# Inverting the recurrence's triangular systems as compact 32x32 blocks, both directions per step

## The chip, the cores and the metric

The kernel runs as one program on one core of a Trainium2 chip. The metric is the device time of one execution in microseconds (us). The core has a matrix engine (PE, with PEld for its weight loads), a vector engine (DVE), an activation engine (ACT), a general engine (POOL) and a queue for transfers (SP). Each engine works through its own list of instructions in the order in which they were issued. One engine waits for another through semaphores, counters that an instruction raises as it ends.

## The reference

A backbone of two layers runs 128 context tokens and 256 latent tokens through SwiGLU blocks, layer norms and a mixer with three branches: grouped attention, differential attention and a bidirectional recurrence (RWKV-7). The change is in the third branch:

```python
def _rwkv_scan(S0, r, w, kk, a, k, v, reverse):
    def step(S, inp):
        r_t, w_t, kk_t, a_t, k_t, v_t = inp
        sa = jnp.einsum('bhvk,bhk->bhv', S, -kk_t)
        S = S * w_t[:, :, None, :] + sa[..., None] * (kk_t * a_t)[:, :, None, :] + v_t[..., None] * k_t[:, :, None, :]
        return S, jnp.einsum('bhvk,bhk->bhv', S, r_t)
...
    for d in range(2):
        a_h, w_h = heads(a), heads(decay)
        S, o = _rwkv_scan(state0[:, d].astype(f32), rh, w_h[:, :, d], kk, a_h[:, :, d], k_h[:, :, d], vh, reverse=(d == 1))
```

There are eight heads of 64 channels, and each direction has its own decay and rate. The outputs are the two token streams, new keys and values of both attentions and the recurrence's state.

## The kernel before

The recurrence isn't run token by token. Time is cut into six chunks of CH = 64 tokens (NQ = 6), the eight heads into four tiles of two (NB = 4, tile j holds heads on partitions 0 to 63 and 64 to 127). Within a chunk the dependence of each token on the earlier ones of the chunk is a triangular system, and the kernel computes its 64x64 inverse. The chunks of a tile are then chained by four scan steps with that inverse. For one tile there are 6 chunks x 2 directions x 2 heads = 24 systems.

For each tile, in each of the two layers, the work is:

- `gram(j, p)`, p = 0 to 3: three chunks of one direction each. PE multiplies keys with queries and keys into two banks, `own` and `swapped`; ACT copies one half of each `own` block to `lt` (L1981, "the gram copy"); DVE masks the rest into `gr` (L2730, L2732).
- `turn_tok`: PE turns keys into token order; ACT copies them.
- The inverse, which is built level by level. `first_level` (DVE L2741) masks `lt` with the pattern of blocks of size 1; `turn_start` (PE) transposes that; `first_level_done` (DVE L2747, L2750) adds the identity to both forms, `xi` (the inverse) and `xt` (its transpose). Then come levels n = 1 to 5, for blocks of 2, 4, 8, 16 and 32. Per level and direction: POOL masks `lt` into `ltm` (L2246, 384 columns); PE multiplies `ltm` with `xi` (`lx_quads`); ACT copies the result to `tl` (L1991); PE multiplies once with `xt` (`u_quads`, for `xi`) and once the other way round (`ut_quads`, for `xt`); DVE adds the first to `xi` (`add_u`, L2756) and the second to `xt` (`add_ut`, L2766, or the copy L2764 at the last level). The last level needs `xt` alone.
- The scan of the tile before (s = j - 1), four steps of `scan_right`, `scan_solve`, `scan_update`, put between the pieces above, and that tile's group norm (`tile_sums`, `tile_var`, `tile_gate`).
- The preparation of the next tile (j + 1): decays and rates (PE L1342 and L1352, ACT L1928 and L1937), sums (DVE L2681), exponentials (ACT L1961 to L1974), keys and queries (DVE L2699, L2708, L2714, L2715), decayed keys (DVE L2722, L2723).

A matrix product on 64x64 blocks is issued by `quads` (L1309): one matmul for each of the two heads, each on its own rows of the array, both into one bank. In the trace each float32 matmul leaves two records. The two directions of a level are staggered: while one is in its copy or its addition, PE works on the other (`level_lx0_u1`, `level_u0_lx1`, `level_ut`):

```python
def level_u0_lx1(j, n):
    u_ready(j, n, 0)
    lx_ready(j, n, 1)
    for q in range(NQ):
        uu = u_quads(j, n, 0, q) if n < NL else ut_quads(j, n, 0, q)
        lx = lx_quads(n, 1, q)
```

The order of the work on each engine is written out by hand in the loop `for j in range(NB)`, once for each engine. Nothing reorders it, so a copy or an addition that stands behind others in that list waits for them. Outside the recurrence the kernel is dense 128x128 matmuls (L905 to L907) on weights that stream in.

Of the kernel before, what the change touches and what calls it, by code (L numbers as in the profile page):

```python
# [17 lines left out]
ALU = mybir.AluOpType  # L18
# [59 lines left out]
CO_MASK = CO_LEV + 2 * len(LEVELS) * CH  # L78
# [6 lines left out]
def shape_constants():  # L85
# [19 lines left out]
    for d in range(2):  # L105
        a, b = (s, t) if d == 0 else (t, s)
        for n, size in enumerate(LEVELS):
            m = (a // (2 * size) == b // (2 * size)) & (a // size % 2 == 0) & (b // size % 2 == 1)
            o = CO_LEV + (2 * n + d) * CH
            c[:, o:o + CH] = m  # L110
# [5 lines left out]
    c[:, CO_ID64:CO_ID64 + CH] = s == t  # L116
    for g in range(32):
# [139 lines left out]
def build(nc, I, O):  # L257
# [17 lines left out]
        "lt_ready": 16, "ltm_ready": 40, "max_done": 48, "merged_done": 16, "n_ready": 24, "o_done": 4, "o_read": 4,  # L275
# [6 lines left out]
        "tile_sum": 6, "tl_done": 40, "tl_ready": 40, "tok_ready": 16, "tok_sums": 6, "tok_t": 16, "u_done": 32,  # L282
        "ut_done": 40, "var_ready": 3, "vt_done": 1, "vtok_ready": 4, "vtok_t": 4, "weighted_done": 24, "xf_ready": 24,
        "xhi_ready": 32, "xi_ready": 40, "xi_t": 8, "xm_ready": 32, "xt0_ready": 8, "xt_ready": 48, "z_ready": 8}
# [12 lines left out]
    with glob:  # L297
# [78 lines left out]
        with ExitStack() as mix:  # L376
# [27 lines left out]
            with ExitStack() as ph:  # L404
# [5 lines left out]
                with ExitStack() as same:  # L410
# [8 lines left out]
                tl = sb("tl", [128, 2 * NQ, CH], ctx=ph)  # L419
# [13 lines left out]
                ksq = (guc[:, 0, :], guc[:, 1, :], tl[:, 0:NQ, :].rearrange("p q s -> p (q s)"),  # L433
                       tl[:, NQ:2 * NQ, :].rearrange("p q s -> p (q s)"))
# [46 lines left out]
        ltm_ready, xt0_ready, xt_ready, xi_t, xi_ready = (  # L481
            sem(n) for n in ("ltm_ready", "xt0_ready", "xt_ready", "xi_t", "xi_ready"))
        tl_done, tl_ready, u_done, ut_done = (sem(n) for n in ("tl_done", "tl_ready", "u_done", "ut_done"))
# [2518 lines left out]
```

## Time and profile before

| what | value |
|---|---|
| median of 3 runs | 2526.09 us (2523.46 to 2530.59) |
| profiled execution, first to last instruction | 2519.7 us |
| median less that span | 6.4 us |
| PE busy | 2379.6 us (94%), 23632 matmul records |
| DVE busy | 1368.0 us (54%) |
| ACT busy | 1031.8 us (41%) |
| POOL busy | 342.1 us (14%) |
| chain that ended last | PE 84%, DVE 9%, issue 2%, ACT 2% |

The page gives the span of the profiled execution and no further time of it, so the 6.4 us are what lies around the span, as far as that execution was like the median one. The shares of busy time are averages over the whole program: the recurrence fills some 190 us of each layer, from 718 to 912 us in layer 1 and from 1957 to 2151 us in layer 2, and there the engines stand differently to one another than in the dense parts.

### The profile page before, as it was taken

How to read it: one execution, taken by the hardware profiler on the slowest of the kernel's cores; microseconds unless marked ns; L12 is line 12 of the kernel's file. 1: busy time of each engine (PE TensorE's matmuls, PEld its weight loads, DVE VectorE, ACT ScalarE, POOL GpSimd, SP SyncE). 2: the span in 40 equal slices, each digit the busy share in tenths (PEclk: the TensorE clock that was granted, in tenths of full speed). 3: DMA queues.
4: the chain of work that ended last, by engine and by line, in shares of the span. 5: the costliest groups of instructions: out<-in, count | busy, mean ns of one | idle time of the engine just before them, and what ended most of it. 6: DMA issues, size and time to landing. Idle time of an engine off the chain costs nothing.

```text
span 2519.7 us, 56070 instructions
## 1 busy us (share of the span) xinstructions
PE 2379.6 (94%) x23632; PEld 2228.4 (88%) x23632; DVE 1368.0 (54%) x2301; ACT 1031.8 (41%) x1677; POOL 342.1 (14%) x330
## 2 busy tenths in 40 slices
PE   6999999999988889999999999999999788899998
PEld 5899989889977779999988999998899777899998
DVE  3434456477488756344443334655765876554444
ACT  3333244355644435333343333444556343353332
POOL 0000032000033304000120001320000433130002
PEclk8999999999989999999999999999999899999999
DMA  8875634332300023554457765343333000344442
GB/s 286 265 229 177 216 98 134 92 95 85 105 15 4 29 56 114 172 176 125 150 179 237 221 186 182 99 114 91 95 85 92 3 4 29 89 117 128 127 120 86
DMA packets 468550, 309.32 MB, mean 123 GB/s; under 512 B 15330, under 2 KB 427468, under 8 KB 468172
## 3 DMA queue, kind: packets, MB, share of 16 engines
q1 hardware_dynamic: 468032, 305.65, 40.4%
q8 instruction: 187, 3.06, 0.5%
q14 instruction: 63, 0.52, 0.1%
q10 hardware_dynamic: 268, 0.09, 0.0%
HBM read 302.30 MB, written 3.41 MB: 121 GB/s over the span
## 4 chain that ended last, share of the span: by engine, by line
PE 84%; DVE 9%; issue 2%; ACT 2%; DMA 1%; POOL 1%; SPq 1%; DVEq 0%; ACTq 0%; POOLq 0%
PE acc L905 22%; PE acc L906 21%; PE acc L907 21%; PE pb L1309 4%; PE acc L1309 2%; PE pb L982 2%; PE pb L990 1%; DMA raw<-in_ffn_w_in 1%; PE pb L1236 1%; PE pb L997 1%; DVE w_lo L2328 1%; DVE merged L2631 1%; PE pb L905 1%; DVE gr L2732 1%; PE acc L969 0%
## 5 line engine op out<-in xcount | busy, mean ns | idle before, releaser
L905 PE MATMUL acc<-xm_hi,w_hi 128*128 128x384 f32 x2288 | 784.5, 343 | 28.7 <-DVE xm_lo L2338 24.4
L2328 DVE TENSOR_TENSOR w_lo<-raw,w_hi 128x1024 fp32r<-128x1024 f32 (+2 forms) x432 | 533.9, 1236 | 509.5 <-ACT w_hi L1733 501.0
L907 PE MATMUL acc<-xm_hi,w_lo 128*128 128x384 f32 x2288 | 771.3, 337 | 0.0
L906 PE MATMUL acc<-xm_lo,w_hi 128*128 128x384 f32 x2256 | 760.6, 337 | 0.0
L1733 ACT ACTIVATE w_hi<-raw 128x1024 fp32r<-128x1024 f32 (+2 forms) x432 | 446.2, 1033 | 316.1 <-PE acc L907 224.0
L905 PEld LDWEIGHTS acc<-xm_hi,w_hi 128*128 128x128 f32 x2288 | 434.7, 190 | 59.8 <-issue 49.0
L907 PEld LDWEIGHTS acc<-xm_hi,w_lo 128*128 128x128 f32 x2288 | 434.3, 190 | 0.0
L906 PEld LDWEIGHTS acc<-xm_lo,w_hi 128*128 128x128 f32 x2256 | 428.9, 190 | 0.5
L905 PE MATMUL acc<-h_hi,w_hi 128*128 128x384 f32 x704 | 238.9, 339 | 0.0
L907 PE MATMUL acc<-h_hi,w_lo 128*128 128x384 f32 x704 | 237.1, 337 | 0.0
L906 PE MATMUL acc<-h_lo,w_hi 128*128 128x384 f32 x704 | 237.1, 337 | 0.0
L1768 ACT ACTIVATE sa<-acc 128x384 f32<-128x384 f32 x88 | 43.3, 492 | 428.9 <-PE acc L907 428.7
L2192 POOL TENSOR_TENSOR ln_sum<-x 128x384 f32<-128x384 f32 x12 | 17.6, 1470 | 879.4 <-DVE x L2354 879.2
L905 PEld LDWEIGHTS acc<-h_hi,w_hi 128*128 128x128 f32 x704 | 132.4, 188 | 5.0 <-issue 5.0
L906 PEld LDWEIGHTS acc<-h_lo,w_hi 128*128 128x128 f32 x704 | 132.4, 188 | 0.0
L907 PEld LDWEIGHTS acc<-h_hi,w_lo 128*128 128x128 f32 x704 | 132.4, 188 | 0.0
L2440 DVE TENSOR_TENSOR hf<-sa,acc 128x384 f32<-128x384 f32 x88 | 48.8, 555 | 145.9 <-PE acc L907 138.3
L2246 POOL TENSOR_TENSOR ltm<-lt,cst 128x384 f32<-128x384 f32 x80 | 83.7, 1047 | 145.1 <-PE pb L1309 86.4
L2354 DVE SCALAR_TENSOR_TENSOR x<-acc,modv,x 128x128 f32<-128x128 f32 x88 | 32.7, 413 | 108.3 <-PE acc L907 108.1
L1309 PE MATMUL pb<-xi,ltm 64*64 64x64 f32 x1920 | 79.2, 229 | 11.0 <-POOL ltm L2246 4.7
L1309 PE MATMUL pb<-xt,tl 64*64 64x64 f32 x1920 | 79.8, 223 | 5.9 <-issue 5.8
L1991 ACT ACTIVATE tl<-pb 128x384 f32<-128x384 f32 x80 | 39.2, 491 | 111.8 <-PE pb L1309 111.5
(394 smaller groups left out, 3472.9 us busy)
## 6 DMA issues: line engine op xcount, KB each, us to landing
raw<-in_ffn_w_in SPq DMA_DIRECT2D x176, 512.0 KB, 4.1
modw<-in_w_mod SPq DMA_DIRECT2D x69, 1024.0 KB, 6.4
raw<-in_w_in SPq DMA_DIRECT2D x114, 512.0 KB, 4.1
raw<-in_ffn_w_out SPq DMA_DIRECT2D x64, 512.0 KB, 3.8
raw<-in_w_up SPq DMA_DIRECT2D x24, 512.0 KB, 3.6
raw<-in_ffn_w_out SPq DMA_DIRECT2D x26, 384.0 KB, 3.2
raw<-in_w_out SPq DMA_DIRECT2D x16, 512.0 KB, 4.0
modx<-in_w_mod SPq DMA_DIRECT2D x3, 1024.0 KB, 9.3
```

The costliest lines, as they stand in the source:

```text
L905: pe.matmul(out, lhs[0], rhs[0], start=first, stop=False)
L906: pe.matmul(out, lhs[0], rhs[1], start=False, stop=False)
L907: return pe.matmul(out, lhs[1], rhs[0], start=False, stop=last)
L982: mm = pe.matmul(pb[2 if late else 1][32 * k:32 * k + 32, :], cond_at(Q - (LATE_Q if late else PRE_Q), 4 * r + k), slot[:, k, :], start=r ...
L1309: mm = pe.matmul(out[HALVES[1 - i] if cross else hp], lhs[hp], rhs[hp], start=start, stop=stop, skip_group_check=True)
L1733: done(act.activation(w_hi[:, c % SPL, 0:w], raw[:, c % RAW, 0:w], ACT.Copy), hi_done)
L1768: freed(l, act.activation(sa[:, j % 2, :], gbank(ka)[:, 0:TOK], ACT.Silu), ka)
L1991: done(act.activation(tl[:, NQ * d:NQ * d + NQ, :].rearrange("p q s -> p (q s)"), lx_bank(n, d)[:, 0:TOK], ACT.Copy), tl_ready)
L2246: done(pool.tensor_tensor(ltm[:, u, :], lt[:, u, :], over(cst[:, o:o + CH], NQ), ALU.mult), ltm_ready)
L2328: done(dve.tensor_tensor(w_lo[:, c % SPL, 0:w], raw[:, c % RAW, 0:w], w_hi[:, c % SPL, 0:w].bitcast(F32), ALU.subtract), lo_done)
L2354: ins = dve.scalar_tensor_tensor(out=x[:, m, a:b], in0=gbank(key)[:, a:b], scalar=modv[:, 3 * s + 2, m, gi:gi + 1], in1=x[:, m, a:b], op0= ...
L2440: freed(l, dve.tensor_tensor(hf[:, j % 2, :], sa[:, j % 2, :], gbank(kb)[:, 0:TOK], ALU.mult), kb)
```

## The change

The 64x64 inverse is no longer built in five levels of 64-wide blocks. Only its two 32x32 diagonal blocks are, in four levels; the remaining off-diagonal block ("the corner") is made by two more products at the end.

- **Blocks.** `xi`, `xc` (the transpose, in the place of `xt` during the levels), `ltm` and `tl` are 32 columns wide for each chunk instead of 64. A bank of 384 columns holds all 12 chunks of both directions, so a level is one product (`level_lx`, 48 matmuls of 32x32x32), one ACT copy, one product (`level_u`, 48 matmuls), one DVE addition, and one DVE transpose of 32x32 blocks (`STREAM_TRANSPOSE`), which takes the place of the second product (`ut_quads`) and its addition. The four matmuls of a chunk lie on four different 32-row groups.
- **First level.** DVE masks, adds the identity and transposes, 192 columns each, for each direction. `turn_start` and `first_level_done` are gone.
- **Masks.** POOL makes those of all four levels at once: for each direction one operation of 192 and one of 576 elements a partition.
- **Corner.** PE `corner_first` (24 matmuls), ACT copy of 192 columns, PE `corner(j, 0)` and `corner(j, 1)` (24 each), an ACT copy of 192 columns each; POOL `place` writes the diagonal blocks to `xt` with zeros beside them (2 operations).
- **Gram.** The half of `own` that is inverted is issued as 32-wide pieces: 24 matmuls for each `gram` instead of 12.
- **Order.** On every engine's list the pieces of both directions fall together.

For one tile that makes 456 matmuls of the inverse in the place of 384, and 96 in the place of 48 in the grams. On DVE, 14 operations (six of 192 columns, eight of 384) stand in the place of 24 of 384. On ACT, 4 copies of 384 and 3 of 192 columns stand in the place of 10 of 384. On POOL, 4 masks (1536 elements a partition in all) and 2 placings stand in the place of 10 masks (3840 elements).

```diff
-LEVELS = (1, 2, 4, 8, 16, 32)
+BL = CH // 2
+LEVELS = (1, 2, 4, 8, 16)
 NL = len(LEVELS) - 1
+XR = NL + 2
+QUARTERS = tuple(slice(32 * g, 32 * g + 32) for g in range(4))
...
-                xi = sb("xi", [128, 2 * NQ, CH], ctx=ph)
-                ltm = sb("ltm", [128, 2 * NQ, CH], ctx=ph)
+                xc = sb("xc", [128, 2 * NQ, BL], ctx=ph)
+                xi = sb("xi", [128, 2 * NQ, BL], ctx=ph)
+                ltm = sb("ltm", [128, NL, 2 * NQ, BL], ctx=ph)
...
-                            quads(own[:, at], bt[:, d, q * CH:(q + 1) * CH], both, True, True)
+                            quads(own[:, 2 * CH * e + CH:2 * CH * e + 2 * CH], bt[:, d, q * CH:(q + 1) * CH], ar[:, j % 2, d, q, 1, :],
+                                  True, True)
...
+                    def blocks(out, lhs, rhs):
+                        for g in QUARTERS:
+                            mm = pe.matmul(out[g], lhs[g], rhs[g], start=True, stop=True, skip_group_check=True)
+                        return mm
+                    def level_lx(j, n):
+                        if n == 1:
+                            pe.wait_ge(gram_read, since(l, gram_read, 4 * j + 4))
+                        pe.wait_ge(ltm_ready, since(l, ltm_ready, 4 * j + (3 if n == 1 else 4)))
+                        pe.wait_ge(xi_ready, since(l, xi_ready, XR * j + n + 1))
+                        for u in range(2 * NQ):
+                            mm = blocks(pb[0][:, u * BL:(u + 1) * BL], ltm[:, n - 1, u, :], xi[:, u, :])
+                        mm.then_inc(tl_done, 1)
+                    def level_u(j, n):
+                        pe.wait_ge(tl_ready, since(l, tl_ready, NL * j + n))
+                        pe.wait_ge(xt_ready, since(l, xt_ready, XR * j + n + 1))
+                        for u in range(2 * NQ):
+                            mm = blocks(pb[2][:, u * BL:(u + 1) * BL], xc[:, u, :], tl[:, u, :])
+                        mm.then_inc(u_done, 1)
...
-                    def level_lx(j, n, d):
-                        act.wait_ge(tl_done, since(l, tl_done, 2 * NL * j + 2 * (n - 1) + d + 1))
+                    def level_lx(j, n):
+                        act.wait_ge(tl_done, since(l, tl_done, NL * j + n))
+                        done(act.activation(tl[:, :, :].rearrange("p u s -> p (u s)"), pb[0][:, 0:2 * NQ * BL], ACT.Copy), tl_ready)
...
+                    def masks(j, d):
+                        pool.wait_ge(lt_ready, since(l, lt_ready, 4 * j + 2 * d + 2))
+                        for n0, n1 in ((1, 2), (2, NL + 1)):
+                            form = [128, n1 - n0, NQ, BL]
...
-                    def add_ut(j, n, d):
...
+                    def add_u(j, n):
+                        whole = xi[:, :, :].rearrange("p u s -> p (u s)")
+                        dve.wait_ge(u_done, since(l, u_done, NL * j + n))
+                        done(dve.tensor_tensor(whole, whole, pb[2][:, 0:2 * NQ * BL], ALU.add), xi_ready)
+                        done(dve.transpose(xc[:, :, :].rearrange("p u s -> p (u s)"), whole), xt_ready)
...
-                        for n in range(2, NL + 1):
-                            level_lx0_u1(j, n)
-                            level_ut(j, n - 1, 1)
...
-                            level_u0_lx1(j, n)
-                            level_ut(j, n, 0 if n < NL else 1)
+                        level_u(j, 2)
+                        if nxt:
+                            prepare_norm(j + 1)
+                        level_lx(j, 3)
+                        if old:
+                            tile_sums(s)
+                        level_u(j, 3)
```

ACT's list in tile 1, from the copy of `tl` at level 1 to the one at level 2 (`aa<-acc` are the next tile's rates, `osum` the scan's output, `zi` and `eh` exponentials of the next tile, `sld` a state). Before:

```order
L1991 ACTIVATE tl<-pb 128x384
L1961 ACTIVATE cs<-zi 128x384
L1966 ACTIVATE sg<-sg 128x384
L2008 ACTIVATE sld<-acc 128x2x64
L1937 ACTIVATE aa<-acc,half_bias 128x384 x2
L2004 ACTIVATE osum<-acc 128x384
L1991 ACTIVATE tl<-pb 128x384
L1970 ACTIVATE zi<-zi 128x384
L1974 ACTIVATE eh<-lam 128x6
L1991 ACTIVATE tl<-pb 128x384
```

and now:

```order
L1991 ACTIVATE tl<-pb 128x384
L1960 ACTIVATE cs<-zi 128x384
L1965 ACTIVATE sg<-sg 128x384
L2016 ACTIVATE sld<-acc 128x2x64
L1936 ACTIVATE aa<-acc,half_bias 128x384 x2
L2012 ACTIVATE osum<-acc 128x384
L1969 ACTIVATE zi<-zi 128x384
L1973 ACTIVATE eh<-lam 128x6
L1991 ACTIVATE tl<-pb 128x384
```

The exponentials of `zi` and `eh` stood between the level's two copies; now they stand ahead of its only one. The two rates stand ahead of it as before.

PE's list in the same tile, from the scan's last update to the second product of level 3:

```order
L1320 MATMUL acc<-gr,sas 64x64 x4
L1415 MATMUL pb<-xi,ltm 32x32 x48
L1363 MATMUL acc<-cmix,lora_a 128x384 x2
L1415 MATMUL pb<-tl,xc 32x32 x48
L1178 MATMUL acc<-cst,ln_st 64x128 x6
L1415 MATMUL pb<-xi,ltm 32x32 x48
L1563 MATMUL acc<-osum,cst 128x384
L1566 MATMUL acc<-guc,cst 128x384
L1415 MATMUL pb<-tl,xc 32x32 x48
```

Before, the rates `acc<-cmix,lora_a` (whose results ACT's `aa<-acc` takes) stood ahead of the first product of level 2; they now stand behind it.

## Rows read from the trace of the kernel before

**Rows 1.** Stretches: span, busy PE, PEld, DVE, ACT, POOL (instructions), clock, DMA share, GB/s

```profile
783.40:806.70 23.30, 20.62 (x712) 17.35 (x709) 18.75 (x35) 13.77 (x26) 11.42 (x12) 1.00 0.02 5
874.30:895.80 21.50, 18.80 (x644) 16.63 (x634) 10.46 (x20) 7.36 (x13) 6.00 (x6) 0.92 0.25 78
```

**Rows 2.** Chain that ended last, in order of time, tiles 1 and 3: start, us, what

```profile
783.05 0.85 PE acc L1352 x4
...
785.44 0.81 PE acc L1167 x12
786.24 0.84 PE acc L1562 x2
787.09 0.65 PE acc L1565 x2
...
801.08 0.57 DVE xt L2766
...
881.25 1.94 issue
```

**Rows 3.** Whole program, groups by line, with mean ns of one instruction

```profile
L2246 POOL TENSOR_TENSOR ltm<-lt,cst 128x384 f32<-128x384 f32 x80 | 83.7, 1047 | 145.1 <-PE pb L1309 86.4 <-issue 39.7 <-ACT lt L1981 16.4
...
L2766 DVE TENSOR_TENSOR xt<-xt,pb 128x384 f32<-128x384 f32 x72 | 39.9, 554 | 8.8 <-PE pb L1309 5.5
L1991 ACT ACTIVATE tl<-pb 128x384 f32<-128x384 f32 x80 | 39.2, 491 | 111.8 <-PE pb L1309 111.5
```

**Rows 4.** Timeline of PE, products of one level: start, us, instruction, count

```profile
744.21 0.22 PE L1309 MATMUL pb<-tl,xt 64*64 64x64 f32 x2
744.23 0.23 PE L1309 MATMUL pb<-xi,ltm 64*64 64x64 f32 x2
744.27 0.23 PE L1309 MATMUL pb<-tl,xt 64*64 64x64 f32 x2
...
744.86 0.87 PE L1309 MATMUL pb<-xt,tl 64*64 64x64 f32 x24
```

**Rows 5.** Timeline of PE's weight loads at the same place

```profile
744.11 0.14 PEld L1309 LDWEIGHTS pb<-tl,xt 64*64 64x64 f32 x2 [0.17 <-issue]
744.12 0.14 PEld L1309 LDWEIGHTS pb<-xi,ltm 64*64 64x64 f32 x2
744.16 0.14 PEld L1309 LDWEIGHTS pb<-tl,xt 64*64 64x64 f32 x2
```

**Rows 6.** Timeline of DVE, tiles 1 and 3

```profile
797.46 0.65 DVE L2714 TENSOR_TENSOR gg<-eh 128x5 f32<-128x5 f32 x1
...
857.68 1.33 DVE L2741 TENSOR_TENSOR xt<-lt,cst 128x384 f32<-128x384 f32 x1
```

**Rows 7.** Timeline of ACT, tile 1, around level 2

```profile
783.97 1.19 ACT L1937 ACTIVATE aa<-acc,half_bias 128x384 f32<-128x384 f32 x2 [0.58 <-PE acc L1352]
...
786.24 0.52 ACT L1970 ACTIVATE zi<-zi 128x384 f32<-128x384 f32 x1
```

**Rows 8.** Gram copies of ACT: the last one of tiles 0, 1 and 3

```profile
732.90 0.33 ACT L1981 ACTIVATE lt<-pb 128x192 f32<-128x192 f32 x1 [2.55 <-PE pb L1309]
...
774.41 0.33 ACT L1981 ACTIVATE lt<-pb 128x192 f32<-128x192 f32 x1 [2.46 <-PE pb L1309]
...
866.24 0.33 ACT L1981 ACTIVATE lt<-pb 128x192 f32<-128x192 f32 x1 [1.54 <-PE pb L1309]
```

**Rows 9.** Timeline of DVE: where tiles 0, 1 and 3 are through

```profile
762.34 0.36 DVE L2730 TENSOR_TENSOR gr<-pb,cst 128x192 f32<-128x192 f32 x1
...
806.67 0.36 DVE L2730 TENSOR_TENSOR gr<-pb,cst 128x192 f32<-128x192 f32 x1
...
895.22 0.56 DVE L2764 COPY xt<-pb 128x384 f32<-128x384 f32 x1
```

**Rows 10.** Stretches of 3 us where the clock falls; columns as in Rows 1

```profile
729.00:732.00 3.00, 1.53 (x32) 1.38 (x32) 2.83 (x6) 0.49 (x1) 0.00 (x0) 0.50 0.00 0
...
858.00:861.00 3.00, 1.29 (x42) 1.29 (x44) 2.83 (x6) 0.24 (x2) 0.59 (x1) 0.82 0.00 0
```

More of the change, by code:

```diff
@@ L534, in gram_banks, with side, on_diagonal @@
             return (pb[2], pb[3]) if p % 2 == 0 else (pb[0], pb[1])
-        def lx_bank(n, d):
-            return pb[d + 2 * (1 - n % 2)]
-        def u_bank(n, d):
-            return pb[d + 2 * (n % 2)]
+        def side(d):
+            return slice(NQ * d, NQ * d + NQ)
+        def on_diagonal(d):
+            return lt[:, side(d), BL * d:BL * d + BL]
         def gbank(key):
@@ new lines, in level_u, with corner_first @@
+                    def level_u(j, n):
[4 more added lines that the diff above has]
+                        mm.then_inc(u_done, 1)
+                    def corner_first(j):
+                        pe.wait_ge(xi_ready, since(l, xi_ready, XR * j + XR))
+                        for q in range(NQ):
+                            for d in range(2):
+                                for h in range(2):
+                                    of, to = QUARTERS[2 * h + d], QUARTERS[2 * h + 1 - d]
+                                    mm = pe.matmul(pb[0][to, q * BL:(q + 1) * BL], lt[of, NQ * d + q, BL * (1 - d):BL * (1 - d) + BL],
+                                                   xi[of, NQ * d + q, :], start=True, stop=True, skip_group_check=True)
+                        mm.then_inc(corner_t, 1)
@@ new lines, in corner @@
+                    def corner(j, d):
+                        pe.wait_ge(corner_ready, since(l, corner_ready, 3 * j + 1))
+                        pe.wait_ge(xt_ready, since(l, xt_ready, XR * j + XR))
+                        for q in range(NQ):
+                            for h in range(2):
+                                of, to = QUARTERS[2 * h + 1 - d], QUARTERS[2 * h + d]
+                                at = slice(q * BL, q * BL + BL)
+                                pe.matmul(pb[1 - d][to, at], toff[of, q, :], xc[of, NQ * d + q, :], start=True, stop=True,
+                                          skip_group_check=True)
+                                mm = pe.matmul(pb[1 - d][of, at], cst[of, CO_ID32:CO_ID32 + BL], xc[of, NQ * d + q, :],
+                                               start=True, stop=True, skip_group_check=True)
+                        mm.then_inc(corner_t, 1)
@@ L1629, in _ @@
                             scan_right(s, 1)
-                        turn_start(j, 0)
-                        if old:
                             scan_solve(s, 1)
@@ L1655, in _ @@
                             scan_update(s, 3)
+                        level_lx(j, 2)
                         if nxt:
@@ L2120, in _ @@
                             exp_halves(g1)
-                        level_lx(j, 5, 1)
+                        corner(j, 0)
+                        corner(j, 1)
                         if old:
@@ L2284, in _ @@
                             decay(2 * j + 3)
-                        for n in range(1, NL + 1):
-                            mask(j, n, 0)
-                            mask(j, n, 1)
-                            if n == 3 and nxt:
-                                rate(2 * j + 2)
-                                rate(2 * j + 3)
-                            if n == 4 and nxt:
-                                keys(2 * j + 2)
+                        masks(j, 0)
+                        masks(j, 1)
                         if nxt:
+                            rate(2 * j + 2)
+                            rate(2 * j + 3)
+                            keys(2 * j + 2)
                             keys(2 * j + 3)
+                        place(j, 0)
+                        place(j, 1)
                         if old:
@@ new lines, in first_level @@
+                        link(dve.tensor_tensor(mine, on_diagonal(d), over(cst[:, o:o + BL], NQ), ALU.mult))
+                        done(dve.tensor_tensor(mine, mine, over(cst[:, CO_ID32:CO_ID32 + BL], NQ), ALU.add), xt_ready)
+                        done(dve.transpose(xi[:, side(d), :].rearrange("p q s -> p (q s)"), mine.rearrange("p q s -> p (q s)")), xi_ready)
+                    def add_u(j, n):
[3 more added lines that the diff above has]
+                        done(dve.transpose(xc[:, :, :].rearrange("p u s -> p (u s)"), whole), xt_ready)
```

239 lines of the change are left out of this document (82 added, 157 removed).

## The prediction

> **What bounds the kernel now.** The dense parts are untouched, so I read only the recurrence, and first by stretches: in tile 1 of layer 1 the levels take 23.3 us in which DVE is busy for 18.75 us and PE for 20.62 us [rows 1]. Both are nearly full, so the second view decides, the chain that ended last. It runs mostly over PE up to 797 us, and from there to 813 us over DVE alone, one 0.57 us operation after the other, the level additions among them [rows 2]. So in the second half of a tile DVE is the bound, and PE, busy as it looks, waits for it. In tile 3, which has no next tile to prepare, DVE is busy for only 10.46 us of 21.5 [rows 1]: there the chain product, copy, product, addition sets the time.
>
> I price the stretch from the last gram copy of a tile to the first masking that belongs to the next one. Before, it is 774.41 to 806.67 = 32.3 us in tile 1, 732.90 to 762.34 = 29.4 us in tile 0, and, to the last write of `xt`, 866.24 to 895.78 = 29.5 us in tile 3 [rows 8, 9].
>
> **What a step on PE costs.** The new product has 48 matmuls, 96 records, on four row groups. Now four 64x64 parts of the array are in use when two directions are issued together: pairs of records start at 744.21, .23, .27, so four records each 58 ns, 14.6 ns a record [rows 4]. A part is thus renewed every 58 ns for 64 columns. With two parts only, 24 records take 0.87 us with 0.22 us of tail: 27 ns a record, 55 ns a part [rows 4]. The time is per part and goes with the columns, so for 32 columns I take half, 29 ns a part, 7.3 ns a record with four parts: 96 x 7.3 = 0.70 us, with the tail **0.95 us**. The upper bound is that a record doesn't come faster than the 14.6 ns seen: 96 x 14.6 = 1.40, with tail **1.65 us**. Which one depends on how fast PE can issue. For the fast end speaks the start of a burst: four weight loads begin within about 0.02 us, then none for 0.04 us [rows 5], so the loads wait for the array and not for the issue. I take 0.95 us. Both are at the clock of 2.4 GHz.
>
> **The sum for tile 1**, from the last gram copy:
> - First level. DVE masks gram in 0.95 us, then three operations of 192 columns at 0.36 (192 columns from the bank: 0.36 [rows 9]) = 1.1. POOL has a mask of 192 and one of 576 elements; at 1.05 us for 384 [rows 3] that is 0.5 + 1.6 us, starting with the copy, and a masking of `lt` on DVE beside POOL took 1.33 us [rows 6], where 0.56 is usual. I take 0.8 us of waiting, and 0.45 for copy and semaphores: **3.3 us**.
> - Four levels, each two steps (1.9), a copy of 0.49 + 0.06 [rows 3], an addition of 0.55 + 0.05 (as L2766 [rows 3]): 3.05 x 4 = **12.2 us**. The transpose isn't in it: it comes after the addition, which alone the next product needs, and is over while that product and its copy run. Its cost shows in no row; I take that of a 384-column addition, 0.56; half of that changes nothing, and up to 1.5 us stays covered.
> - PE's other work in the list. Rate 0.85, norm 0.81, sums 0.84 + 0.65 [rows 2], and the scan's last steps and the tile's variance, 2.5 us by my reading of the list. Of these 5.7 us the part behind a product whose copy is awaited is hidden, 0.55 us each four times: **3.5 us**.
> - ACT's queue at level 2. The copy now stands behind the two rates (1.19), the scan's output (0.49), and the exponentials `zi` and `eh` (0.52 [rows 7] and, for 6 columns, some 0.2), and the rates can begin only after PE's 0.85, which stands behind the product. Product to copied is then 0.85 + 1.19 + 0.49 + 0.73 + 0.49 + 0.2 = 3.95 us instead of 0.55: **3.4 us**, of which the 0.85 is already counted above: **2.6 us**.
> - DVE's tail after level 4: from 797.46 to 806.67 it never idles and runs five level operations of 0.57 there [rows 6, 9]; the other 6.3 us stay: **6.3 us**, with the last transpose 0.6 ahead. The corner (2.3 us on PE and ACT: 72 matmuls, 1.1 us with tails, three copies of about 0.35) lies beside this tail and costs nothing; without the tail it would cost its 2.3.
> Sum 28.5 us against 32.3: **-3.8 us**. Tile 2 has the same list: -3.8.
>
> **Tile 0** has no scan and no norm of an old tile (3.3 us less), but the clock is at half where its levels begin (0.50 at 729 to 732 us [rows 10]), which I price at +1.9: 27.1 against 29.4, **-2.3**. **Tile 3** has neither rates nor next keys: 3.3 + 12.2 + 3.0 of other PE work + 0.8 of ACT's queue + corner 2.3 = 21.6; of the 29.5 before some 2.5 are PE waiting for nothing that the profile shows (1.94 in one piece [rows 2]), while the weights' stream returns (DMA share 0.25 over the stretch [rows 1]), and I leave them in: 24.1, **-5.4**. In the half of a tile before the last gram copy `turn_start` leaves PE's chain (-0.7), the gram gets 24 more records (+0.35) and the first level grows from 0.57 to 1.1 us on DVE (+0.45): nothing.
>
> A layer gives -15.3, two layers -31. Against it stands the **clock**: in the row at 858 us PE was busy for 1.29 of 3 us, and in it the granted clock fell from 2.4 to 1.2 GHz (mean 0.82) [rows 10]. After the change PE waits about 3 us for ACT's queue in each of tiles 0 to 2. I allow one such fall in each tile, 1.4 us each: +11. So **-20 us**: the profiled span of 2519.7 goes to 2500, and the median of 2526.1, which lies 6.4 above that span, to **2506 us**.
>
> **The rivals.**
> - *Issue sets the pace* (1.65 us a step). Eight steps x 0.7 = 5.6 us a tile, 45 us in all, less 10 that fall into waits anyway; PE is busier then, so without the falls of the clock: -31 + 35 = +4, **2530 us**. For it: 14.6 ns is the fastest sustained pace the trace shows, and every step has 192 instructions. Against it: rows 5. It decides from about 13 ns a record. A middle pace of 11 ns gives about 2518.
> - *The clock falls and stays*, the case on the other side. PE now stands still in every level for copy and addition, 1.15 us of 3.05. If the clock falls to 1.2 GHz in the levels, each step costs 0.65 more (5.2 us a tile) and the grams, scans and norms on the chain about 5 us more; in all eight tiles +80, in the six without tile 0's slow start, for two thirds of the time, +40: 2526 - 31 + 40 = **2535 us**. For it: at 729 us PE was busy for 1.53 of 3 us and the clock stood at 0.50 [rows 10]. Against it: in the levels of tile 1, where PE waited between products too, it stood at 1.00 throughout [rows 1].
> - *Row groups take turns.* If four 32-row parts don't run side by side but as slowly as the two-part rows (27 ns a record), a step is 2.8 us, 1.85 more, eight a tile: +118 - 31 = **2613 us**. Against it: in rows 4 and 5 the two heads' matmuls, on different rows and into one bank, start together. The Trainium skill, "TensorE: Matmul & The Clock Gate", section on the 56 ns, says that matmuls never start less than about 25 ns apart however few columns they have. By that rule a step would be 96 x 25 = 2.4 us and the kernel slower; the trace disagrees as far as records on different parts go (14.6 ns), and agrees with it if it is meant for one part (29 ns).
> - *The chain moves to something I hold for covered*, DVE against POOL's long mask, or the corner. Each microsecond a tile costs 8; with three, **2526 us**, no change.
>
> **How the numbers follow.** Main case 0.56 (2492 to 2518 by its bounds: the fall of the clock between 0 and 1.5 times a tile, step 0.9 to 1.2 us); issue pace 0.17; clock 0.09; turns 0.04; cover lost 0.14. A measurement of this kernel tells about 0.3%, 7.6 us, from no change. Faster: the main case, and a part of the others, 0.60. Same: cover lost and part of issue pace, 0.19. Slower: the rest, 0.21. The range takes in the main case, cover lost and issue pace: 2488 to 2534; outside are the turns and half of the clock's case.
>
> **What would show it.** Right: 32x32 records that start 7 to 8 ns apart, a step of 0.9 to 1.0 us; DVE busy 6 to 7 us less a tile; PE idle in tile 1 with ACT's copy of `tl` as releaser, about 3 us at level 2; chain no longer on DVE between level 1 and 4. Wrong: records 14 ns or more apart; a granted clock of 0.50 over whole tiles; a transpose longer than 1.5 us; `gr` of the next tile waiting for the corner.

## The result, and the profile after

The changed kernel takes **2604.94 us** (median of 4 runs, 2603.72 to 2610.7), the kernel before 2526.90 us in the same comparison; the ratio is 1.031 (95% interval 1.0295 to 1.0326). I had forecast 2506 us, faster. The profiled execution spans 2604.3 us against 2519.7.

The recurrence holds nearly the whole difference. In layer 1 it takes 39.2 us more; in layer 2, from the first gram masking to the end of the last tile, 246.3 us (from 2000.27) against 202.1 (from 1959.18), 44.2 us more; the spans differ by 84.6. First the kernel before (the whole stage of layer 1, then tile 1), columns as in [rows 1]:

```profile
718.40:919.80 201.40, 169.80 (x5640) 149.32 (x5640) 145.27 (x272) 79.49 (x162) 64.72 (x68) 0.95 0.07 18
762.34:806.67 44.33, 38.89 (x1404) 34.06 (x1404) 35.74 (x69) 21.13 (x43) 16.44 (x18) 1.00 0.02 4
```

The changed kernel, the same two, then the levels of tile 1 alone, from the first LX product to the corner's first:

```profile
718.70:959.30 240.60, 180.20 (x6600) 149.27 (x6600) 118.99 (x232) 71.73 (x150) 42.84 (x52) 0.75 0.06 16
769.15:825.03 55.88, 41.95 (x1654) 34.10 (x1650) 29.31 (x58) 19.20 (x40) 11.24 (x14) 0.81 0.02 4
789.70:816.26 26.56, 18.27 (x893) 14.96 (x891) 9.14 (x18) 9.43 (x19) 4.40 (x6) 0.82 0.02 4
```

DVE lost the 6.4 us a tile that I expected, and it isn't the bound any more. But PE has 250 records more in tile 1, and the mean granted clock of the stage fell from 0.95 to 0.75. Against [rows 8, 9]: from the last gram copy (783.87) to the next tile's masking (825.03) it now takes 41.2 us, where it took 32.3 and I forecast 28.5. The 12.7 us too few are 2.5 at the first level, 8.3 in the levels, 1.9 at the end. The part of the tile ahead of that stretch, which I had put at no change, takes 14.7 us (769.15 to 783.87) against 12.1 [rows 8, 9]. Tiles 0 to 3 of the layer take 6.3, 11.6, 8.0 and 13.2 us more than before, each from its first masking to the next tile's (tile 3 to the end of the stage), where I had forecast 2.3, 3.8, 3.8 and 5.4 less.

PE's products in that stretch, by the timeline (start, length, record, count, in brackets the idle time before and what ended it):

```profile
789.70 1.50 PE L1415 MATMUL pb<-xi,ltm 32*32 32x32 f32 x96
793.53 1.02 PE L1415 MATMUL pb<-tl,xc 32*32 32x32 f32 x96 [1.42 <-ACT tl L1991]
...
797.71 0.67 PE L1415 MATMUL pb<-xi,ltm 32*32 32x32 f32 x55 [0.33 <-issue]
...
809.02 1.02 PE L1415 MATMUL pb<-tl,xc 32*32 32x32 f32 x96
810.85 1.10 PE L1415 MATMUL pb<-xi,ltm 32*32 32x32 f32 x96
812.60 0.37 PE L1415 MATMUL pb<-tl,xc 32*32 32x32 f32 x19
814.53 1.01 PE L1415 MATMUL pb<-tl,xc 32*32 32x32 f32 x77 [1.56 <-issue]
```

A step takes 1.02 us at 2.4 GHz (forecast 0.95) and 1.50 at 1.2 GHz. Two kinds of gap stand between: those that another engine ends, and two in the middle of a step, "issue": idle time for which the profile shows nothing that was waited for. Level 2 waited 3.17 us for ACT's copy, as I had foreseen (about 3). DVE's and ACT's timelines in tile 1 show the masked product beside POOL's long one, which I had allowed for, and the square root behind the corner, for which DVE waited and which I had not.

```profile
785.28 1.33 DVE L2751 TENSOR_TENSOR xc<-lt,cst 128x192 f32<-128x192 f32 x1
...
822.20 0.19 DVE L2807 RECIPROCAL gnr<-gnr 128x6 f32<-128x6 f32 x1 [2.37 <-ACT gnr L2025]
```

```profile
820.54 1.28 ACT L2025 ACT_TABLE_LOAD   x1
821.84 0.27 ACT L2025 ACTIVATE gnr<-acc,lam 128x6 f32<-128x6 f32 x1
```

The clock in stretches of 3 us; it stands at 1.2 GHz (0.50) where PE did nothing or little, and falls where PE waits for ACT or DVE (in the third row PE had been idle from 799.23 to 802.39, and from 798 to 801 the clock was still 1.00):

```profile
732.00:735.00 3.00, 0.00 (x0) 0.00 (x0) 2.83 (x6) 0.00 (x0) 0.00 (x0) 0.50 0.00 0
744.00:747.00 3.00, 1.22 (x4) 0.07 (x2) 0.00 (x0) 1.63 (x3) 0.00 (x0) 0.50 0.00 0
801.00:804.00 3.00, 1.61 (x98) 1.54 (x100) 0.00 (x0) 2.66 (x6) 0.54 (x2) 0.56 0.00 0
```

Before, 744 to 747 stood at 1.00 with PE busy for 2.74 us.

### The profile page after: what moved, and what is told of

Its sections match the earlier page's. It is cut to its first block, busy times and chain, and to the rows that moved or that the text cites. A ratio compares the mean times of both kernels' runs of the same rounds, so it can differ in the third digit from the quotient of the medians.

```text
span 2604.3 us, 59482 instructions
## 1 busy us (share of the span) xinstructions
PE 2404.0 (92%) x25552; PEld 2232.7 (86%) x25552; DVE 1316.8 (51%) x2221; ACT 1016.6 (39%) x1653; POOL 298.8 (11%) x298
## 3 DMA queue, kind: packets, MB, share of 16 engines
q1 hardware_dynamic: 468032, 305.44, 39.2%
## 4 chain that ended last, share of the span: by engine, by line
PE 87%; DVE 7%; ACT 3%; issue 2%; DMA 1%; POOL 0%; SPq 0%; DVEq 0%; ACTq 0%; POOLq 0%
PE acc L916 22%; PE acc L917 21%; PE acc L918 21%; PE acc L1320 3%; PE pb L1415 3%; PE pb L993 2%; PE pb L1001 1%; PE pb L1320 1%; PE pb L1247 1%; PE pb L1008 1%; PE acc L1178 1%; DVE w_lo L2337 1%; PE pb L916 1%; DVE xc L2751 1%; DVE merged L2640 1%
## 5 line engine op out<-in xcount | busy, mean ns | idle before, releaser
L1415 PEld LDWEIGHTS pb<-tl,xc 32*32 32x32 f32 x3072 | 38.5, 130 | 55.9 <-ACT tl L1991 39.1
L1415 PE MATMUL pb<-tl,xc 32*32 32x32 f32 x3072 | 43.5, 218 | 42.5 <-ACT tl L1991 31.5
L2759 DVE TENSOR_TENSOR xi<-xi,pb 128x384 f32<-128x384 f32 x32 | 17.7, 554 | 128.2 <-PE pb L1415 128.2
L2260 POOL TENSOR_SCALAR sg<-sg 128x384 f32<-128x384 f32 x16 | 8.5, 533 | 525.7 <-ACT sg L1927 524.7
```

Source lines behind the costliest of these rows:

```text
L1415: mm = pe.matmul(out[g], lhs[g], rhs[g], start=True, stop=True, skip_group_check=True)
```

## The experiments

Four theories stood: **A**, the clock at 1.2 GHz; **B**, waits that come from the order of the queues (B2) and from both directions being one step (B1); **C**, the instructions of PE don't arrive fast enough; **D**, POOL's long product slows DVE's first level. Where I give a difference it is between medians. All except the last four are edits of the changed kernel.

**Idle PE filled (e_fill).**

```
+def fill(n):
+    for _ in range(n):
+        pe.matmul(pb[3][:, 384:512], ident, cst[:, 0:128], start=True, stop=True, ...)
 ...
+fill(4)            # 3 to 12 of them in each wait
 level_u(j, 1)
```

> Idle TensorE filled: 20 to 35 extra matmuls a tile (128x128 with 128 columns, into 128 unused columns of a bank, nobody reads them) stand in TensorE's waits between the inverse's steps; every wait, queue and dependency stays as in the changed kernel. Theory A (the clock: the changed kernel's TensorE stands still between serial steps, and the granted clock is at 1.2 GHz in some 119 of the 240 us of a layer's recurrence, where before it was in some 20 of 201): with the waits filled the clock is at 2.4 GHz nearly throughout, a step of 96 records takes 1.02 us everywhere where 1.50 is common now, and the time falls by 25 to 45 us, to 2560 to 2580. Theory B (the serial chain and the order of the queues cost, the clock little): at most 10 us less; 2595 to 2610. If the extra matmuls themselves run past the waits they fill, both are hidden and the time rises: 2610 to 2640.

Measured 2619.99 us (ratio to before 1.0363, 1.0333 to 1.0393), 15 us more: the third of the cases. Its timeline of PE in tile 0:

```profile
750.20 0.86 PE L1415 MATMUL pb<-xi,ltm 32*32 32x32 f32 x78 [0.18 <-issue]
...
754.04 0.67 PE L1415 MATMUL pb<-tl,xc 32*32 32x32 f32 x54 [1.40 <-issue]
...
757.93 0.46 PE L1415 MATMUL pb<-xi,ltm 32*32 32x32 f32 x33 [1.25 <-issue]
...
761.64 0.58 PE L1415 MATMUL pb<-tl,xc 32*32 32x32 f32 x26 [1.76 <-issue]
```

The clock part came true in part: more steps ran at 1.02 us, the mean clock of layer 1's recurrence rose from 0.75 to 0.85 and that of the program from 0.933 to 0.954. The time didn't follow: issue gaps ahead of level products grew from 6.8 to 13.4 us in the layer, in tile 0 one every 3.8 us. Theory A fell as the cause of the whole, and C came up. The test isn't a clean one, as the fillings are instructions too: 216 records more in the layer, by the rate measured below an estimated 12 us in both layers.

**Halves (e_halves), order (e_order), POOL (e_pool).**

```
 def level_lx(j, n):             # e_halves; U, ACT's copy, DVE's addition and transpose alike
-    for u in range(2 * NQ): ... pb[0] ... ; mm.then_inc(tl_done, 1)
+    for d in range(2):
+        for q in range(NQ): ... pb[d] ... ; mm.then_inc(tl_done, 1)
 ...
+level_lx(j, 1)                  # e_order, ACT
 copy_tok(j, 1, 1); scan_right(s, 3)
-level_lx(j, 1)
 ...
+pool.wait_ge(xi_ready, ...)     # e_pool, ahead of the product for levels 2 to 4
```

> One part of the change undone: the blocks stay 32x32 with four levels, corner and transposes, and all other work keeps its place in every queue, but each step is two halves again, one for each direction (48 records, a bank of its own, copy, addition and transpose of 192 columns). Theory B1 (both directions as one step leave nothing to work on while a step's copy or addition is under way): a level's four waits of TensorE (some 0.7 us after the products, 0.7 and more after the addition) are half covered by the other direction, about 1 us a level less, 32 levels: 25 to 40 us from that and some 10 to 20 from the clock, so 2545 to 2575. Theory A alone (clock) would show the same sign, but only with the share of 2.4 GHz up. Rival (the added instructions of ACT and DVE, each with a fixed cost, and the queue waits decide): 2600 to 2615.

> The change kept whole, only the order of independent work altered: ACT's copy of level 1 ahead of the ktok and rs copies, that of level 2 ahead of the two rate activations and the output copy, the square root and its two table loads ahead of the corner; on DVE the third scan copy ahead of the second direction's first level; on TensorE the root's expansion ahead of the next tile's first gram part. Theory B2 (the waits that came from queue order cost what the trace shows of them: 2.8 us at the first level, 1.4 less 0.7 at level 1, 3.2 less 0.7 at level 2, 1 to 2 at the tile's end, in three tiles of four): 5 to 7 us for each of six tiles, 30 to 42 us less: 2562 to 2575. Theory A: the clock stays as it is since the time between steps is as empty as before, 15 us at most: 2590 to 2605.

> Only POOL's long mask product of each direction (576 columns, 1.55 us) waits until DVE's first level of that direction is done; nothing else is altered. Theory D (the first masked product on DVE takes 1.33 to 1.53 us in place of 0.36 because POOL's long product runs beside it, and all of it lies on the path to level 1): DVE's L2751 falls to about 0.4 us, 1 us for each of eight tiles, 5 to 9 us less: 2596 to 2600. If the product is not on the path, or POOL's later end delays level 2 or the rates: no difference, 2602 to 2608.

Measured: e_halves 2608.13 (1.0309, 1.0291 to 1.0326), no gain, as its rival said; B1 fell as a cause by itself. e_order 2581.92 (1.0205, 1.0187 to 1.0222), 23 us less where B2 wanted 30 to 42. e_pool 2598.00 (1.0274, 1.0258 to 1.0289), 7 us less, as D said; the masked product on DVE, by its line (minimum, median, maximum in ns), in the changed kernel and in e_pool:

```profile
L2751 DVE TENSOR_TENSOR xc<-lt,cst x16: 357/1076/1526, 726.7 to 2183.7; 128x192 f32<-128x192 f32 x16
```

```profile
L2753 DVE TENSOR_TENSOR xc<-lt,cst x16: 357/359/831, 724.6 to 2176.3; 128x192 f32<-128x192 f32 x16
```

In e_order the waits for ACT's `tl` went and issue gaps stood in their place, in the level steps of tile 1:

```profile
790.92 0.59 PE L1415 MATMUL pb<-tl,xc 32*32 32x32 f32 x46 [1.58 <-issue]
...
802.76 0.26 PE L1415 MATMUL pb<-xi,ltm 32*32 32x32 f32 x8 [2.59 <-issue]
```

The level stretch of tile 1 in e_fill, e_halves and e_order, against 26.56 us for 893 records, hardly moves, whatever wait is taken out:

```profile
794.87:821.93 27.06, 23.19 (x937) 19.78 (x936) 9.52 (x19) 9.43 (x19) 5.29 (x7) 0.88 0.02 4
```

```profile
787.68:815.17 27.49, 19.13 (x892) 15.60 (x890) 10.66 (x26) 10.12 (x23) 4.77 (x6) 0.75 0.02 4
```

```profile
786.70:813.24 26.54, 19.72 (x891) 16.09 (x891) 10.82 (x22) 12.46 (x24) 4.83 (x6) 0.77 0.02 4
```

**Instructions fewer and more.** e_wide makes each level block with two 64x64 weights, e_extra adds 48 one-column products to a wait, e_cut takes 48 products a tile out of the gram half and the corner (POOL and ACT take over a part), e_order_pool joins the two that helped.

```
-mm = blocks(pb[0][...], ltm[:, n - 1, u, :], xi[:, u, :])      # e_wide
+mm = quads(pb[0][...], ltm[:, n - 1, v:v + 2, :]..., xi[:, u, :], True, True)
 ...
+for _ in range(2 * NQ):                                        # e_extra, before level_u(j, 2)
+    blocks(pb[3][:, 384:385], cst[:, 0:BL], cst[:, 0:1])
```

> Work changed so that the output is not the reference's: in the level steps each 32-column block is made by 2 products of 64x64 weights instead of 4 of 32x32, with the same sources, destinations and waits; a step has 48 records and 48 weight loads instead of 96 and 96. Theory C (TensorE's instructions are the bound: the trace shows them arriving in packets of 16 KB, never closer together than about 3.3 us, some 256 instructions of TensorE each, and idle time before records of one step with nothing waited for, up to 1.8 us): 768 instructions a tile less are 3 packets, 10 us a tile where the supply binds; the idle time put down to issue goes from the level steps, and the time falls by 35 to 70 us, to 2535 to 2570. Theory A+B (clock and serial waits): only the products' own time, some 0.3 us in each of 64 steps, less: 2582 to 2592.

> The opposite: 48 products of one column (32x32 weights, unused target) more in each tile, put behind the second LX step where TensorE waits 3.2 us for ACT's copy anyway; 96 records and 96 weight loads more, about 0.7 us of TensorE. Theory C (instruction supply): 192 instructions are three quarters of a packet, 2.5 us a tile later on, although they stand in a wait: 10 to 22 us more, 2615 to 2627, and more issue time in later steps. Theory A+B: hidden in tiles 1 and 2, 0.7 us in some of the others: 2603 to 2609.

> Fewer instructions of TensorE with the result kept: in the gram half one product of 128 columns as before the change and one 32x32 block written over it (24 products a tile less), and in the corner no products by the identity, POOL copies these rows instead (24 a tile less); 192 instructions a tile less in all, more work on POOL and two more copies on ACT. Theory C: three quarters of a packet a tile, 10 to 20 us less: 2584 to 2595. Theory A+B: TensorE is not the bound there, POOL and ACT have more to do at the tile's end: 2600 to 2612.

> The two that helped together: the altered order of independent work and POOL's long product behind DVE's first level. If their gains add (23 and 7 us): 2573 to 2577. Theory C: what the first frees the instruction supply takes back in part, so less than the sum, 2576 to 2582, with more issue time than in either.

Measured: **e_wide** 2665.19 (1.0531, 1.0509 to 1.0552), a miss and no test: two parts of the array in place of four made a step of 48 records 2.77 us at 1.2 GHz, in place of 1.50. **e_extra** 2624.39 (1.0367, 1.0346 to 1.0387), 19.5 us more for 0.7 us of PE a tile put into a wait of 3.2, within C's 10 to 22. **e_cut** 2605.94 (1.0299, 1.0282 to 1.0315): nothing gained, against C's 10 to 20. **e_order_pool** 2569.69 (1.0158, 1.0136 to 1.0181), 35 us less, where the sum is 30 and C wanted less than the sum: that part of C's forecast missed. The issue gaps did grow, before level products to 17.2 us in a layer against 6.8 in the changed kernel (the waits of PE: total, times, longest):

```profile
PE pb L1415 <- issue: 17.2, 17, 2.3
```

```profile
PE pb L1415 <- issue: 6.8, 7, 1.6
```

**The supply by itself (e_stream).**

```
 if n == 1:
     pe.wait_ge(gram_read, ...)
+    if j == 0:
+        for _ in range(12 * 2 * NQ):
+            blocks(pb[3][:, 384:384 + BL], cst[:, 0:BL], cst[:, 0:BL])
```

> The supply measured by itself: in the first tile of each layer, before level 1, 576 independent products of 32x32 (an unused target, the same shape as a step's, in all twelve steps' worth: 1152 records and 1152 weight loads) that wait for nothing. Theory C (a packet of 16 KB, 256 instructions, at most every 3.3 us): 2304 instructions are 9 packets, so after a first burst at the pace of a step the stretch runs in bursts with issue gaps between, 26 to 30 us in all, and the time rises by 45 to 55 us for the two layers (4.5 us of each stretch lie in a wait): 2650 to 2660. Rival (the pace of the records, 8.4 ns at 2.4 GHz to 12.6 at 1.2 GHz, holds for a long stream too): 12 to 15 us in all, 2620 to 2630.

Measured 2678.07 (1.0584, 1.0568 to 1.06); the stretch runs from 734.56 to 765.5, 31 us where C said 26 to 30 and the rival 12 to 15. In the timeline of PE:

```profile
734.56 3.20 PE L1415 MATMUL pb<-cst 32*32 32x32 f32 x223 [3.25 <-DVE gr L2744]
739.32 1.93 PE L1415 MATMUL pb<-cst 32*32 32x32 f32 x128 [1.56 <-issue]
742.77 1.93 PE L1415 MATMUL pb<-cst 32*32 32x32 f32 x128 [1.52 <-issue]
746.50 1.93 PE L1415 MATMUL pb<-cst 32*32 32x32 f32 x128 [1.80 <-issue]
...
761.14 1.93 PE L1415 MATMUL pb<-cst 32*32 32x32 f32 x128 [1.80 <-issue]
764.87 0.65 PE L1415 MATMUL pb<-cst 32*32 32x32 f32 x33 [1.80 <-issue]
```

and the transfers of the 26 us from 739 to 765 (queue: packets, MB, share):

```profile
q8 instruction: 7, 0.11, 1.9%
```

The same queue over the whole program, in the changed kernel and in e_stream:

```profile
q8 instruction: 202, 3.31, 0.5%
q8 instruction: 220, 3.60, 0.6%
```

This is the cause in its plainest form. After a burst of 223 records come groups of exactly 128, seven of them between the starts at 739.32 and 764.87 (25.55 us), and seven instruction packets of 16 KB: one packet every 3.65 us, **28.5 ns a record**. Over the program e_stream has 2304 records and as many weight loads more than the changed kernel, and 18 packets more: 256 instructions each, which are 128 records and their 128 weight loads. The Trainium skill, "Perfetto Trace Analysis", section on the lifecycle of an instruction, says that instructions are of 64 bytes; 256 of them are 16 KB, and this trace agrees. The time rose by 73 us where C said 45 to 55. In layer 1 tile 0 took 32.8 us more, 29.5 of them ahead of its first level product: the wait that I had set off against the stretch hid about 1.5 us of it and not 4.5. The next tile took 4.3 more. The clock stood at 1.2 GHz in the stretch; but in tile 0's levels it did so in the changed kernel too.

**Combined, and where fewer records help.** e_all is e_order_pool with e_cut, e_gram_cut with its gram part alone, e_all_halves adds the halves to e_all.

> The altered order, POOL's product behind the first level, and the 192 instructions a tile less, together. Theory C: once the queue waits are out of the way TensorE's instructions are what the level steps wait for, so the cut that gained nothing alone now gains three quarters of a packet a tile: 10 to 20 us under the kernel with order and POOL alone, 2550 to 2562. Theory A+B: no more than the products' own time, 0.3 us a tile, and POOL's added copies: 2565 to 2575.

> As the kernel with the altered order and POOL's product moved, with the gram half's 96 instructions a tile less alone (the corner as in the change). Theory C: a third of a packet a tile, 5 to 10 us less than 2570: 2560 to 2566. Rival: nothing, 2567 to 2573.

> The kernel with order, POOL and cut, its steps in halves again by direction. Theory C: the instruction count is the same, so what the halves cover the supply takes back: within 6 us of the kernel without halves. Theory B1: the halves gained nothing alone since queue waits held both directions; without these, 15 to 30 us less.

Measured 2571.25 (1.0166, 1.0151 to 1.0181), 2570.74 (1.0168, 1.0153 to 1.0184) and 2559.34 (1.0123, 1.0106 to 1.014). The cuts failed a second time, against C's forecasts of 2550 to 2562 and 2560 to 2566: they lie in the gram half and the corner, ahead of and behind the levels. PE takes up instructions ahead, but no more than about that burst of 223 records, so what is saved outside a dense stretch doesn't help inside it; that reading fits, no run isolates it. The halves gained 12 us, between what C and B1 said. e_all_halves is the fastest version with 32x32 blocks and the reference's result.

**Half the records within the levels (e_pairs, e_pairs_order, e_before_pairs).** Each product here covers two neighbouring blocks with the weights of the first, so the result isn't the reference's; the columns are the same in all.

```
-for u in range(2 * NQ):
-    mm = blocks(pb[0][:, u * BL:(u + 1) * BL], ltm[:, n - 1, u, :], xi[:, u, :])
+for u in range(0, 2 * NQ, 2):
+    mm = blocks(pb[0][:, u * BL:(u + 2) * BL], ltm[:, n - 1, u, :], xi[:, u:u + 2, :]...)
```

> Work changed so that the output is not the reference's: each product of a level step takes the 64 columns of two neighbouring blocks with the weights of the first, so a step has 48 records of 64 columns in place of 96 of 32, on the same four row groups, with the same columns in all, sources, targets and waits. Theory C (28.5 ns a record with its weight load is what the instructions allow; 893 records in the level stretch of tile 1 took 26.6 us): 384 records a tile less, 10.9 us by that rate, of which 7 to 11 can be had before the chain of copies and additions binds: 55 to 85 us less, 2520 to 2550. Theory A+B (clock, serial waits): the columns are the same, so 0 to 8 us less: 2597 to 2605.

> The same pairs together with the altered order and POOL's product behind the first level. Theory C: without the supply's limit the queue waits count in full, 3 us and more a tile: 20 to 35 us less than with pairs alone, 2490 to 2520, which is what my sum gave for the change. Theory A+B: 2562 to 2570, as without pairs.

> The kernel before with the same device: LX and U products take 128 columns of two neighbouring chunks with the weights of the first, 216 records a tile fewer of 1404, the same columns; its output is not the reference's. If the kernel before also ran close to the supply's rate (31.6 ns a record over tile 1, against 28.5): 2 to 4 us a tile less, 2500 to 2512. If DVE bounds it, as I read from its profile: 2522 to 2529.

Measured: e_pairs 2561.79 (1.0128, 1.0111 to 1.0145), 43 us less, short of 55 to 85; e_pairs_order **2489.60** (0.9843, 0.9828 to 0.9858), 115 us less than the change and 72 less than e_pairs, where 20 to 35 were expected; e_before_pairs 2511.24 (0.9924, 0.991 to 0.9939), 19.5 us under the kernel before. Tile 1's levels in e_pairs_order:

```profile
774.52:791.70 17.18, 13.90 (x506) 10.90 (x506) 11.98 (x22) 10.46 (x22) 4.04 (x5) 1.00 0.02 4
```

and in e_order_pool, the same but for the pairs:

```profile
781.62:806.84 25.22, 16.38 (x891) 13.13 (x891) 11.97 (x22) 12.60 (x24) 6.05 (x7) 1.00 0.02 5
```

Both at 2.4 GHz, with the same DVE work; 385 records fewer make 8.0 us. A paired step takes 0.87 us in place of 1.02, so 1.2 of the 8.0 are the products' own. The same stretch in e_pairs, with half the records and the queues' order as in the change:

```profile
784.00:809.58 25.58, 19.09 (x508) 14.86 (x506) 9.63 (x20) 9.42 (x19) 2.30 (x4) 0.68 0.01 3
```

So C is shown, but it isn't alone. In tile 1 two limits stand at nearly the same height: halving the records alone takes the stretch from 26.56 to 25.58 us, altering order and POOL alone to 25.22, and both together to 17.18. In e_pairs the 3.17 us wait for ACT's copy is still there, and half of the steps run at 1.2 GHz, which is why it fell short. In the whole kernel order and POOL are worth 35 us with all records and 72 with half of them.

**A version that keeps the result (v_turn, v_turn_order, v_turn_apart)**, edits of the kernel before: 64x64 blocks, five levels, UT by DVE.

```
-done(dve.tensor_tensor(mine, mine, lx_bank(n, d)[:, 0:TOK], ALU.add), xt_ready)
+done(dve.transpose(mine, flat(xi, d)), xt_ready)     # levels 1 to 4, level_ut gone there
```

> A version of the kernel before with the reference's result: blocks of 64x64 and five levels as there, but the other orientation of the inverse comes from DVE's transposes of 32x32 blocks (the matrix has only such blocks on its diagonal until the last level), not from products; the products by the identity that start a tile and the crossing of the two heads' halves of the array go too. TensorE has 288 records of 1404 a tile fewer, DVE the same number of operations of 384 columns. Theory C: the kernel before with 216 records fewer gained 19 us, so 12 to 28 us less than before: 2500 to 2515. Against it: the level products lose their four-part mode (27 ns a record in place of 14.6 within a burst), 5 us a tile if the burst's pace and not the supply decides: 2525 to 2560.

> The same with DVE's third scan copy ahead of the second direction's first level, the part of the altered order that can be carried over alone. As it frees TensorE's last scan products from DVE's 1.7 us or more: 1 to 2 us in each of six tiles, 5 to 10 us less than the version without it; if the products then wait for the supply instead, no difference.

> The version with DVE's transposes and altered scan copy, with the reference's result, but LX and U steps issued apart (LX of one direction, LX of the other, U, U), each of 24 records, 0.7 us, so that the copies and additions of one direction lie beside products of the other; ACT's and DVE's work regrouped to match. In v_turn_order a level takes 4.7 us in tile 1 (795.07 to 799.95): two double steps of 1.4 us and two waits of 0.8 to 0.9 us with their tails. Apart, if the waits are covered, 2.9 to 3.4 us a level, four levels, eight tiles: 35 to 55 us less than v_turn_order, 2490 to 2510, below both kernels. If DVE (36 us busy in tile 1 before) or POOL's masks bind instead: 2515 to 2535.

Measured 2551.01 (1.0085, 1.0071 to 1.0099), 2544.33 (1.0055, 1.0042 to 1.0068) and 2535.94 (1.0033, 1.0021 to 1.0045). No product of a level waits for issue, and yet none beats the kernel before; v_turn came out in the case against it, and v_turn_apart 1 us above the worse of its two. In v_turn_order the 48 records of a double step start over 1.4 us, 29 ns each. That is near the 27 ns of two parts of the array [rows 4], the products' own pace and not the supply's; a wait follows:

```profile
795.07 0.33 PE L1309 MATMUL pb<-tl,xt 64*64 64x64 f32 x4 [0.81 <-DVE xi L2736]
...
797.52 0.33 PE L1309 MATMUL pb<-xi,ltm 64*64 64x64 f32 x4 [0.84 <-ACT tl L1975]
```

In v_turn_apart PE waits longest for DVE's scan state `sp` (10.5 us in layer 1), then for DVE's `kt` at the tile's end (6.5) and POOL's masks (5.2). The limit of the supply was taken away; the slower products and the serial chain of copy, addition and mask came in its place, and no run separates the two. I found no version that gives the reference's result and beats both.

## Why the prediction was wrong, by its steps

**What bounds the kernel now.** I read DVE as the bound of a tile's second half and PE as waiting for it. Only half right: 216 records fewer a tile took 19.5 us off the kernel before with DVE unchanged. At 1404 records in 44.33 us, 31.6 ns each, tile 1 already ran close to the 28.5 of e_stream.

**"What a step on PE costs": the step that failed**, though its number was nearly right. 0.95 us was forecast and 1.02 measured, at 8.4 ns a record. But I took the pace of one burst for the pace of a stretch, and from [rows 5] concluded that "the loads wait for the array and not for the issue". That row shows the start of one burst, and e_stream shows that a burst of up to 223 records says nothing of the pace behind it. The row I should have asked for is the instruction queue: packets over a tile against records over a tile.

**"Four levels ... 12.2 us"**, with PE's other work 3.5 and ACT's queue 2.6: 18.3 us by the sum for the levels; 26.56 measured, and 17.18 once the records are half and the order altered. It lacked the line 893 records x 28.5 ns = 25.5 us, or some 23 us with a full burst ahead (e_stream's first 892 records, 734.56 to 757.80); either is larger than all of it. For a whole tile the same line gives 1654 x 28.5 = 47.1 us, above the 40.5 that I forecast for tile 1 (44.3 less 3.8) and above the 44.3 of before. But as a sum of waits and durations it was too small as well: with half the records e_pairs still took 25.58 us there. The price per record isn't to be multiplied out either: by it the 250 records more would be 57 of the 78 us, yet e_cut and e_gram_cut took 96 and 48 of them away and gained nothing. It is a floor of a dense stretch.

**"In the half of a tile before the last gram copy ... nothing"**: 2.6 us more in tile 1 (14.7 against 12.1). I counted 24 records more where a tile's four grams have 96; e_gram_cut, with half of these gone, gained nothing, so the cause of this term stays open.

**First level 3.3 us**: 5.8. DVE's wait beside POOL was in the sum at 0.8 us and showed 0.97 (1.33 against 0.36; e_pool, where POOL's product comes later, has 0.36); not in it was that `scan_update` stands ahead of the first level product on PE and waits for a copy that stands behind DVE's first level (2.8 us at 787.80).

**The corner costs nothing beside the tail**: wrong by 1.9 us a tile. ACT's square root and table load stand behind the corner's copies, and DVE waited 2.37 us for them. Moving these, the two points above and ACT's copies of levels 1 and 2 gave 35 us of the 78 back.

**The clock** was in the sum at 11 us for one fall a tile. It was at 1.2 GHz for about half of the stage (mean 0.75). Raising it in part (e_fill) gained nothing while the supply bound. Where the supply doesn't bind, it counts among the waits: in tile 1's levels 0.68 and 25.58 us in e_pairs, 1.00 and 17.18 in e_pairs_order. No run separates the clock from the queue waits there. How the 78 us split between clock, waits and supply can't be said in one number, since each hides the others.

**The rivals.** "Issue sets the pace" named the mechanism, with a price taken from 14.6 ns, the fastest sustained pace I had seen, and was therefore 75 us short. "The clock falls and stays" came true in its condition and not as the cause. "Row groups take turns", 2613 us, is nearest to the measured time for a reason that isn't so, by luck: records on four row groups start 8.4 ns apart in the burst. The Trainium skill, "TensorE: Matmul & The Clock Gate", section on the 56 ns, says that products never start less than about 25 ns apart; the burst disagrees with it, and the mean over a long stream, 28.5 ns, doesn't. The sum of "The chain moves", three us a tile, should read 2530 and not 2526 (2506 and eight times 3).

## What to carry to other kernels

Count PE's records, not only their array time: where a long stretch of small products is dense, expect no less than records x 28.5 ns beyond the burst that is already there, and put that line into the sum beside the chain. A finer tiling that trades columns for instructions can lose there even if each step is as fast as planned. And when taking out a wait moves nothing, look whether idle time "issue" has grown; two limits of the same height have to be taken out together before either shows its worth.

## What the runs showed of the hardware

- Instructions for PE came as 16 KB packets of 256 (4608 instructions more in e_stream made 18 packets more). In e_stream groups of 128 records started 3.45 to 3.73 us apart; a burst of 223 records ran ahead of the first gap.
- The clock made no difference to the rate of supply in what was run: 28.5 ns a record in e_stream at 1.2 GHz, 28.3 ns in the levels of e_order_pool at 2.4 GHz (25.22 us, 891 records).
- Four row groups of 32 give 8.4 ns a record at 2.4 GHz in a burst, some 13 ns at 1.2 GHz (1.93 us less the tail for 128).
- DVE's transpose takes 0.38 us for 192 columns and 0.58 for 384, two hundredths more than an addition (0.36, 0.56).
